# Weight sums moved from VectorE to GpSimd in two MLPs, and a longer lead for the dense work in two cross-attentions

## The reference

```
h = h + mixer(rms_norm(h, g_mix))
h = h + cross_attention(rms_norm(h, g_x), mem_n, wq, wkv, wo)
h = h + sq_relu_mlp(rms_norm(h, g_mlp), w1, w2)

def cross_attention(h, mem_n, wq, wkv, wo):        # 4 heads of 256, 256 memory rows
    q = h @ wq;  k, v = split(mem_n @ wkv)
    p = softmax(q @ k.T / 16)                      # for each head
    return (p @ v) @ wo

def sq_relu_mlp(h, w1, w2):                        # w1 1024 x 4096, w2 4096 x 1024
    a = relu(h @ w1)
    return (a * a) @ w2
```

## Time and profile before

| | us |
|---|---|
| median of 3 runs | 2250.34 (2250.26 to 2250.8) |
| profiled execution, its own time | 2252.59 |
| span in the profile, first to last instruction | 2249.8 |
| PE busy | 2217.7 (99%) |
| DVE busy | 1454.9 (65%) |
| ACT busy | 975.6 (43%) |
| POOL busy | 14.5 (1%) |

### The profile page before, as it was taken

One profiled execution on the slowest core, in us unless ns is written; L12 is line 12 of the kernel. 1 busy time (PEld: TensorE's weight loads), 2 busy tenths in 40 slices (PEclk: granted clock), 3 DMA queues, 4 the chain that ended last, 5 costly groups with the idle time before them and its releaser, 6 DMA issues. The chain is left out here.

```text
span 2249.8 us, 31744 instructions
## 1 busy us (share of the span) xinstructions
PE 2217.7 (99%) x12112; PEld 1859.3 (83%) x12112; DVE 1454.9 (65%) x2448; ACT 975.6 (43%) x1676; POOL 14.5 (1%) x14
## 2 busy tenths in 40 slices
PE   9999999999999999999999999999999999999998
PEld 7777778888777788888898889998888788799997
DVE  5866565557656556686665767766755647677775
ACT  5444543334445244364554534443323435444443
POOL 0000000000000000200000000000000000000000
PEclk9999999999999999999999999999999999999999
DMA  5655443245545323454344223333233213233331
GB/s 198 188 157 168 136 130 108 94 140 172 171 143 156 105 103 121 129 165 139 110 154 133 85 94 96 111 97 101 94 94 96 86 45 103 84 103 94 94 114 56
DMA packets 136694, 268.14 MB, mean 119 GB/s; under 512 B 21773, under 2 KB 79931, under 8 KB 136160
## 3 DMA queue, kind: packets, MB, share of 16 engines
q1 hardware_dynamic: 136544, 266.13, 37.2%
HBM read 235.37 MB, written 26.77 MB: 117 GB/s over the span
## 5 line engine op out<-in xcount | busy, mean ns | idle before, releaser
L2064 PE MATMUL ps<-t_P0H,t_whi 128*128 128x512 f32 (+1 forms) x1568 | 593.1, 378 | 3.1 <-DVE t_P0L L2425 2.7
L2065 PE MATMUL ps<-t_P0L,t_whi 128*128 128x512 f32 (+1 forms) x1568 | 585.1, 373 | 0.0
L2066 PE MATMUL ps<-t_P0H,t_wlo 128*128 128x512 f32 (+1 forms) x1464 | 553.2, 378 | 0.0
L2207 ACT ACTIVATE t_whi<-t_raw 128x1024 fp32r<-128x1024 f32 (+2 forms) x295 | 300.5, 1024 | 158.3 <-PE ps L2066 156.6
L2380 DVE TENSOR_TENSOR t_wlo<-t_raw,t_whi 128x1024 fp32r<-128x1024 f32 (+2 forms) x289 | 342.3, 1185 | 39.8 <-PE ps L2066 27.5
L2064 PEld LDWEIGHTS ps<-t_P0H,t_whi 128*128 128x128 f32 x1568 | 295.6, 189 | 80.2 <-issue 22.9
L2065 PEld LDWEIGHTS ps<-t_P0L,t_whi 128*128 128x128 f32 x1568 | 295.3, 188 | 55.4 <-issue 1.0
L2066 PEld LDWEIGHTS ps<-t_P0H,t_wlo 128*128 128x128 f32 x1464 | 275.5, 188 | 54.7
L2064 PE MATMUL ps<-t_P1H,t_whi 128*128 128x512 f32 (+1 forms) x548 | 210.2, 384 | 1.4 <-DVE t_X L2546 0.6
L2065 PE MATMUL ps<-t_P1L,t_whi 128*128 128x512 f32 (+1 forms) x548 | 208.5, 380 | 0.0
L2066 PE MATMUL ps<-t_P1H,t_wlo 128*128 128x512 f32 (+1 forms) x524 | 201.1, 384 | 0.0
(11 more groups left out here) (341 smaller groups left out, 3888.9 us busy)
## 6 DMA issues: line engine op xcount, KB each, us to landing
t_raw<-in_wts SPq DMA_DIRECT2D x362, 512.0 KB, 3.5
far<-t_Tb SPq DMA_DIRECT2D x26, 384.0 KB, 3.0
far<-t_Tb SPq DMA_DIRECT2D x16, 512.0 KB, 3.1
t_PTX<-far SPq DMA_DIRECT2D x64, 96.0 KB, 2.8
t_raw<-in_wts SPq DMA_DIRECT2D x16, 384.0 KB, 3.0
t_QKV<-far SPq DMA_DIRECT2D x32, 128.0 KB, 3.3
t_raw<-in_wts SPq DMA_DIRECT2D x13, 256.0 KB, 3.1
t_PTX<-far SPq DMA_DIRECT2D x24, 128.0 KB, 3.8
```

Of the source, the lines that this page charges most:

```text
L2064: e.matmul(s.out, s.sh, s.mh, start=s.first, stop=False, skip_group_check=again)
L2065: e.matmul(s.out, s.sh, s.ml, start=False, stop=False, skip_group_check=again)
L2066: i = e.matmul(s.out, s.sl, s.mh, start=False, stop=s.end, skip_group_check=again)
L2207: e.activation(s.dst, s.raw, ACT.Copy).then_inc(*mark("hi", s.j))
```

## The change

Three edits.

1. `drive` in `cross` gets `lead=6` in place of 2 in both layers, and in layer 1 the ratio 25/6 in place of 13/3.
2. The step `sums` is run by POOL in place of DVE, with the same four operations in the same order, and its signals get a semaphore of their own.
3. In `pair_of_tiles` the emission of steps for the next pair moves: `u0(n + 1)` from after `other(0)` to after the first copy; `low(n + 1, "u0")` from after the second copy to ahead of `other(0)`; `sums(n + 1)` from after T3 to after `other(0)`. For the first pair (n = 2) `low(n, "w1", 3)`, which also starts a load, moves from after the third copy to after `other(0)`.

```diff
-            drive(main(), fill(), 5, 1, lead=2)
+            drive(main(), fill(), 5, 1, lead=6)
         else:
-            drive(main(), fill(), 13, 3, lead=2)
+            drive(main(), fill(), 25, 6, lead=6)
...
             p = product(bx, u["u0"], 0, "B11", True, xf)
             s1 = snap(a0, p, af)
+            if more:
+                u0(n + 1)
             if n == 2:
                 low(n, "u3")
                 low(n, "w0", 2)
                 w2(n, 1)
...
             c11 = add(a0, z, s1, p)
             PB.give(bz, c11)
+            low(n + 1, "u0")
             other(0)
+            if n == 2:
+                low(n, "w1", 3)
             if more:
-                u0(n + 1)
+                sums(n + 1)
             else:
                 ahead(W["n"] - 1)
             p = product(bx, u["u1"], 0, "T2", False, [s1])
             s2 = snap(b0, p, bf)
-            if more:
-                low(n + 1, "u0")
             p7 = product(bv, u["u2"], 0, "T3", True, vf)
-            if more:
-                sums(n + 1)
             other(1)
...
             low(n + 1, "u1", 0)
-            if n == 2:
-                low(n, "w1", 3)
             other(2)
...
 def gpsimd_program(e, steps, at, mark):
...
+        elif s.name == "sums":
+            for k in s.need:
+                if new(k):
+                    e.wait_ge(*at(*k))
+            e.tensor_tensor(s.t, s.a21, s.a22, ALU.add).then_inc(*mark("sum_1", s.id))
+            e.tensor_tensor(s.a21, s.a11, s.a21, ALU.subtract).then_inc(*mark("sum_3", s.id))
+            e.wait_ge(*at("sum_3", s.id))
+            e.tensor_tensor(s.a11, s.t, s.a11, ALU.subtract).then_inc(*mark("sum_2", s.id))
+            e.wait_ge(*at("sum_2", s.id))
+            e.tensor_tensor(s.a12, s.a12, s.a11, ALU.subtract).then_inc(*mark("sums", s.id))
```

More of the change, by code:

```diff
@@ L89 @@
     "final_act": "final_square final_gain",
-    "parts_dve": "part_lo sum_1 sum_2 sum_3 sums c_add combined combined_1 combined_2 combined_3",
+    "parts_dve": "part_lo c_add combined combined_1 combined_2 combined_3",
+    "parts_pool": "sum_1 sum_2 sum_3 sums",
     "parts_act": "part_hi snapped gained",
@@ L2039, in gpsimd_program @@
 def gpsimd_program(e, steps, at, mark):
+    new = fresh()
     for s in steps:
@@ L2385, in vector_program @@
             e.tensor_tensor(s.lo, s.src, s.hi.bitcast(F32), ALU.subtract).then_inc(*mark("part_lo", s.of))
[L2386 to L2395, removed]
         elif s.name == "combine":
```

## The result

The changed kernel takes 2257.22 us (median of 9 runs), the kernel before 2251.44 us (9 runs on the same chip): a ratio of 1.0025, interval 1.0015 to 1.0035. It is slower by about a quarter of a per cent, 5.8 us; the forecast was 12.5 us faster. The profiled execution took 2256.98 us with a span of 2254.7, against 2252.59 and 2249.8, so it shows 4.9 of these 5.8 us.

What follows compares the result with a forecast made beforehand. PE, busy 99% of the span, was taken as the bound, so only its idle or lower-clock time could be won. The terms - 10.4 - 8.1 + 6.0 = -12.5 us gave 2237.8 us from 2250.34, range 2231 to 2250 us.

Steps and rivals of the forecast that it cites:

- First pair of each MLP: PE's 3.29 us wait at other(2) and the lower clock behind it go in both MLPs: 10.4 us removed.
- No cost here: First pair's sums on POOL run some 2 us longer than on DVE, but are hidden behind B11, B21 and other(0).
- Cross-attention: Waits ahead of scores go with six groups ahead: 1.8 us in layer 0, 6.3 in layer 1, together 8.1 us.
- The waits named: Ahead of scores: head 0's 1.61 us in both layers, heads 1 and 2's 1.24 and 1.91 us in layer 1; all go.
- the new wait: Output product behind the last turn in layer 1's cross-attention: its wait grows by 0.76 us, to about 1.0 us idle.
- Steady pairs: B22 starts 0.3 us late behind POOL's sums in pairs 3 to 12 of both MLPs: 20 x 0.3 = 6.0 us lost.
- without the splits four adds take 4 x 1.12 = 4.5 us: POOL's time for a steady pair's four weight sums, before about 1.0 us for which DVE's splits hold them.
- the forecast 0.3: Delay of B22 in each steady pair: 0.9 - 0.68 + 0.1 = 0.3 us.
- d: How much later the weight sums end on POOL than on DVE in a steady pair: 0.9 us.
- the one of 1.28 stands alone: Reason for 0.3 us a steady pair: the trace's single 1.28 us POOL add was set aside against neighbouring rows.
- nine of ten adds: Argument against POOL's sums becoming the bound: only one of the trace's ten POOL adds took 1.28 us.
- the second rival: POOL's sums become the bound at B22 of every steady pair: 25 us lost less 18.5, 2257 us; chance 0.15.

Runs made afterwards that it cites:

- e5: Kernel before with only the first pair's low(n, "w1", 3) moved behind other(0), in both MLPs; 2241.04 us, ratio 0.9953.
- e1: Changed kernel with the four weight sums back on DVE, the rest of the change kept; 2233.61 us, ratio 0.9920.
- e7: Changed kernel with the inputs of all four POOL sums at offsets differing by two elements (8 bytes), 508 of 512 columns; 2237.46 us, ratio 0.9938.
- e4: Kernel before with only the two drive lines of the change (cross-attention dense stream six groups ahead); 2242.22 us, ratio 0.9963.
- e2: Changed kernel with POOL's sum inputs offset by two elements (first two sums) or one (other two), 508 of 512 columns; 2246.31 us, ratio 0.9979.
- e3: Changed kernel with ACT's high half of the next pair's first w2 chunk moved behind the third copy, sums still on POOL; 2237.18 us, ratio 0.9936.
- e6: Kernel before with only the four weight sums moved to POOL, at their old place behind the splits; 2314.88 us, ratio 1.0279.

## Why the prediction was wrong

- **First pair of each MLP, forecast -10.4 us.** Right. Alone (e5) it gave 10.2. In the changed kernel it gave 8.8, because of the new wait of 0.50 us ahead of `other(0)`, which the forecast had not: with the time won ahead of it PE comes earlier to a low half that POOL's longer first sums hold back. "No cost here" for these sums was 1.3 us off; e1 and e7, with shorter sums, have not got that wait.
- **Cross-attention, forecast -8.1 us.** The waits named went, and the new wait is 0.97 us where about 1.0 was forecast. That the table has 8.2 is in part luck. In layer 0 a second wait went too, 0.6 us with overlap and slower start, which the forecast had not seen:

```profile
1177.97 0.35 PE L2116 MATMUL ps<-t_PTbR,t_UPR 128*128 128x256 f32 x1 [0.35 <-DVE t_PTbR L2762]
```

So that cross-attention gave 2.4 us, not 1.8. The front of the kernel, where nothing was changed, hides it: PE comes to it 0.65 us later in this execution (1084.72 for 1084.07 at the same product), and 0.6 later in e4.

- **Steady pairs, forecast +6.0 us.** This is the step that failed, and only by its size. The place (B22), the chain behind it, the 20 repeats and the direction were as told. The term mis-sized is "without the splits four adds take 4 x 1.12 = 4.5 us". They take 1.29 us each and 0.08 between those that wait for each other. The splits hold POOL for (1.61 - 1.29) + (1.75 - 1.29) = 0.78 us rather than 1.0. So POOL is busy for 6.06 us instead of 5.5, and starts 0.15 us behind u0's low half instead of 0.03: 0.68 us on top of the forecast 0.3, and 0.10 more because B22 starts slower after a wait (0.39 us for its first product, 0.29 in e1). That is 1.08 us a pair; measured, 21.6 / 20 = 1.08. Smaller errors cancel here: the forecast took 0.1 us for each of two hand-overs, which take 0.03 and 0.05, and rounded its d of 0.95 down to 0.9.
- **How the wrong value was chosen.** The forecast had both values in the earlier trace rows and took the frequent one: "the neighbouring rows of the same form repeat [...] and the one of 1.28 stands alone". They were alike in shape only, and "nine of ten adds" was a misreading: five of the ten took 1.04 us. The other four are the first of each group, with a shift of 1 element, and took 1.95 us beside a DVE subtraction. The last group, with the shifts 1, 2, 4 and 8, as one line of the kernel before:

```profile
925.56 5.54 POOL L2047 TENSOR_TENSOR t_UP<-t_UP 128x512 f32<-128x512 f32 x4 [3.14 <-DVE t_UP L2694]
```

Since e2 has 1.28 us for a difference of one element with no DVE operation beside it, those 1.95 us are better read as 1.28 and a hold of 0.67 (an estimate) than as 1.04 and a hold of 0.9. What decided was which of these rows matched the sums in their addresses: the one of 1.28. The case that happened is the second rival, at its place and in its direction; it had a chance of 0.15. That its 2257 us is met so closely is luck: the steady pairs cost 21.6 us and not its 25, the other parts gave 17.0 and not 18.5, and the kernel before was 1.1 us slower in these nine runs than in the three that it started from.

- **The Trainium skill** came closer here than the rows that I preferred. "GPSIMD Engine Reference", section "3.1 Elementwise — side-by-side cycle accounting", has 1.96 for a two-input add; measured, 1.29 / 0.69 = 1.87 for the weight sums, and 1.04 / 0.69 = 1.5 only for windowed sums with a shift of 2 or 4.
- **Who holds whom.** The forecast took it that subtractions of two SBUF tiles hold POOL and additions with one PSUM input do not. Both are borne out: 1.61 and 1.75 us beside the splits, 1.30 beside the residual sum at 1374.44. So DVE and POOL do not meet only at semaphores. The Trainium skill, "SBUF — State Buffer", section "SBUF: two separate sides", states it as a lock for a whole instruction, against a DVE operation with two SBUF inputs; the trace agrees, and DVE pays as well (2.38 us for two splits, 1.29 in the earlier trace rows).

## What to carry to other kernels

Before a price is taken from another row of the same operation and shape, ask in what else the two could differ, the operands' offsets above all; a lone outlier may be the row that matches. Where work moves to a slower engine, follow the chain from its last instruction to the product that waits: what decided here was 0.6 us of room, and one ACT step of 1.04 us in that chain that could stand elsewhere (e3). Measure parts apart: two of the three won 18 us between them, and the third took more than that back.

## What the runs showed of the hardware

A POOL operation on two fp32 SBUF inputs, with no DVE operation on two SBUF tiles beside it, is fast where their offsets differ by 8, 16, 24 or 40 bytes: 1.04 us for 512 columns in the windowed sums, 1.09 for 508 and 1.06 for 496 in the weight sums. It is slow for 4, 12, 32 and 64 bytes and for the differences of the weight sums as they stand: 1.28 to 1.30 us for 508 and 512 columns, 1.25 for 496. For the weight sums these are the bytes beyond a difference that is itself a multiple of 32. In every case tried the fast ones are the multiples of 8 that are not multiples of 32. Why, why the fast weight sums take longer than the fast windowed ones, and what other differences do, is not known from these runs.

The clock does not answer every wait of the same length alike. Near 1025 us PE waits 1.5 to 2.0 us in every version, in code that none of the edits touches; it is 2.00 us in the changed kernel and in e3. The windows behind it, of the changed kernel and then of e3:

```profile
1025.70:1029.10 3.40, 3.40 (x18) 3.40 (x18) 3.40 (x7) 1.15 (x2) 0.00 (x0) 0.50 0.98 244
```

```profile
1025.70:1029.10 3.40, 3.40 (x30) 3.22 (x29) 3.40 (x8) 2.37 (x4) 0.00 (x0) 1.00 0.94 296
```

At 0.50 (1.2 GHz) there are 18 matmuls in the window, at 1.00 (2.4 GHz) there are 30. The clock stays at 1.00 there in e2 and e7 too, and this is most of what these three have beyond the others in the table's first column; the rest is a different pace ahead of it. In the same way e5 has the wait of the earlier trace rows ahead of the last scores, 1.92 us, but not the stretch of the earlier trace rows behind it:

```profile
1814.26 0.36 PE L2104 MATMUL ps<-t_E3R 128*128 128x256 f32 x1 [1.92 <-DVE t_ST L2753]
```

```profile
1814.26:1816.12 1.86, 1.86 (x14) 1.82 (x15) 0.62 (x2) 0.00 (x0) 0.00 (x0) 1.00 0.92 244
```

That is its -1.5 us in the stage up to MLP 1, and e6 has the same. So some 1.5 of the 6.3 us that the forecast took back there hung on a fall of the clock that does not come in every execution. Behind the waits of 0.7 to 1.1 us in the changed kernel the clock never fell; behind those of 1.75 to 2.1 us in e6 it fell about every other time.
